# Last stage of a two-block transformer: weights scaled by ScalarE instead of GpSimd, fewer VectorE operations for queries and gates, and transposes and scores issued as one step

## The reference, cut to what matters

```python
def _stick_breaking(q, k, v):          # 16 heads of 64; blocks of 128 queries
        mask = kpos[None, :] < qpos[:, None]
        z = jnp.einsum('bhqd,bshd->bhqs', qb, k).astype(jnp.float32) * scale
        log_beta = jax.nn.log_sigmoid(z)
        log_1mb = jnp.where(mask, jax.nn.log_sigmoid(-z), 0.0)
        suffix = lax.cumsum(log_1mb, axis=3, reverse=True) - log_1mb
        a = jnp.where(mask, jnp.exp(log_beta + suffix), 0.0)
        return jnp.einsum('bhqs,bshe->bhqe', a.astype(v.dtype), v)

def _sb_layer(x, k, v, norm_g, w_in, w_out):
    proj = _rms(x, norm_g) @ w_in
    q, g = jnp.split(proj, [SB_W], axis=-1)
    o = _stick_breaking(q.reshape(...), k, v)
    o = o.reshape(b, s, SB_W) * jax.nn.silu(g)
    return x + o @ w_out
```

## Time and profile before

| | us |
|---|---|
| median of 3 runs (lowest, highest) | 2911.08 (2909.06, 2913.7) |
| the profiled execution, its own time | 2911.05 |
| its span, first to last instruction | 2909.2 |
| TensorE busy | 2843.3 (98%) |
| VectorE busy | 1676.3 (58%) |
| ScalarE busy | 1092.2 (38%) |
| GpSimd busy | 397.3 (14%) |
| mean granted clock of TensorE | 0.995 |

### The profile page before, as it was taken

One profiled execution on the slowest core, in us unless ns is written; L12 is line 12 of the kernel. 1 busy time (PEld: TensorE's weight loads), 2 busy tenths in 40 slices (PEclk: granted clock), 3 DMA queues, 4 the chain that ended last, 5 costly groups with the idle time before them and its releaser, 6 DMA issues.

```text
span 2909.2 us, 34967 instructions
## 1 busy us (share of the span) xinstructions
PE 2843.3 (98%) x14241; PEld 2363.5 (81%) x14241; DVE 1676.3 (58%) x2400; ACT 1092.2 (38%) x1699; POOL 397.3 (14%) x263
## 2 busy tenths in 40 slices
PE   8999999999999999999999999999999899899988
PEld 7888887888888888888887889888888787678777
DVE  5554357675464533555247776555533677768884
ACT  4322244554332322323234454422222444444442
POOL 2000111110100001000011220100001322154430
PEclk9999999999999999999999999999999999999999
DMA  4332332243233233332323233233323222131211
GB/s 141 101 95 94 95 88 73 66 127 106 87 94 97 88 101 98 101 95 87 105 71 92 68 108 118 80 109 95 101 91 98 70 64 69 47 88 59 72 59 51
DMA packets 302240, 258.08 MB, mean 89 GB/s; under 512 B 11367, under 2 KB 299904, under 8 KB 302080
## 3 DMA queue, kind: packets, MB, share of 16 engines
q1 hardware_dynamic: 300704, 254.76, 28.7%
q10 hardware_dynamic: 1024, 1.05, 0.2%
q0 software_dynamic: 352, 0.03, 0.0%
HBM read 252.66 MB, written 2.10 MB: 88 GB/s over the span
## 4 chain that ended last, share of the span: by engine, by line
PE 82%; DVE 10%; ACT 3%; issue 3%; POOL 2%; DMA 1%; ACTq 0%; SPq 0%; POOLq 0%; DVEq 0%
PE PS L1525 26%; PE PS L1527 25%; PE PS L1526 25%; DVE WL L2255 3%; PE PS L1531 2%; PE PS L1770 1%; DVE AF L2701 1%; DVE SM L2619 1%; ACT AF L2129 0%; PE PS L1623 0%; PE PS L1812 0%; PE PS L1811 0%; DVE AR L2711 0%; ACT WH L1872 0%; POOL SM L2869 0%
## 5 line engine op out<-in xcount | busy, mean ns | idle before, releaser
L2255 DVE TENSOR_TENSOR WL<-RAW,WH 128x1024 fp32r<-128x1024 f32 x480 | 617.9, 1293 | 572.9 <-ACT WH L1872 572.6
L1525 PE MATMUL PS<-XH,WL 128*128 128x512 f32 x2256 | 904.4, 401 | 2.9 <-DVE XL L2265 2.9
L1527 PE MATMUL PS<-XH,WH 128*128 128x512 f32 x2256 | 883.3, 392 | 0.0
L1526 PE MATMUL PS<-XL,WH 128*128 128x512 f32 x2256 | 882.1, 391 | 0.0
L1872 ACT ACTIVATE WH<-RAW 128x1024 fp32r<-128x1024 f32 x448 | 465.4, 1044 | 1005.9 <-PE PS L1527 994.6
L1525 PEld LDWEIGHTS PS<-XH,WL 128*128 128x128 f32 x2256 | 425.8, 189 | 101.5 <-issue 12.7
L1527 PEld LDWEIGHTS PS<-XH,WH 128*128 128x128 f32 x2256 | 425.2, 188 | 91.5
L1526 PEld LDWEIGHTS PS<-XL,WH 128*128 128x128 f32 x2256 | 426.3, 189 | 81.1
L1525 PE MATMUL PS<-AR,WL 128*128 128x512 f32 (+1 forms) x1216 | 465.3, 383 | 7.3 <-DVE SC L2599 3.5
L1527 PE MATMUL PS<-AR,WH 128*128 128x512 f32 (+1 forms) x1216 | 460.7, 379 | 0.0
L1526 PE MATMUL PS<-AR,WH 128*128 128x512 f32 (+1 forms) x1216 | 460.6, 379 | 0.0
(11 more groups left out here) (259 smaller groups left out, 3000.0 us busy)
## 6 DMA issues: line engine op xcount, KB each, us to landing
RAW<-in_w_ffn_gu_dram SPq DMA_DIRECT2D x176, 512.0 KB, 3.5
RAW<-in_w_ffn_down_dram SPq DMA_DIRECT2D x80, 512.0 KB, 3.4
RAW<-in_w_mix_in_dram SPq DMA_DIRECT2D x48, 512.0 KB, 4.0
RAW<-in_w_xkv_dram SPq DMA_DIRECT2D x32, 512.0 KB, 3.4
RAW<-in_a_w_in_dram SPq DMA_DIRECT2D x32, 512.0 KB, 4.2
RAW<-in_w_mix_out_dram SPq DMA_DIRECT2D x16, 512.0 KB, 3.4
RAW<-in_w_xq_dram SPq DMA_DIRECT2D x16, 512.0 KB, 4.1
RAW<-in_w_xo_dram SPq DMA_DIRECT2D x16, 512.0 KB, 3.4
```

The lines of the kernel that those rows point to most:

```text
L1525: pe.matmul(o, ll, rh, start=start, stop=False, skip_group_check=skip)
L1526: pe.matmul(o, lh, rl, start=False, stop=False, skip_group_check=skip)
L1527: return pe.matmul(o, lh, rh, start=False, stop=stop, skip_group_check=skip)
L2255: dve.tensor_tensor(l, raw_slot(n), F(h), ALU.subtract).then_inc(sg["wl"].up(n))
```

## The change

The gain scaling moves from GpSimd to ScalarE, as one activation per k tile with the gain as its per-partition factor: 8 operations of 128x128 for a strip, 4 of 128x256 for a unit of values or of others. For the queries of `sb` the factor of the position is no longer multiplied in before the eviction; it goes as factor of each row (RCOL, and its negative NB4) into the sigmoids. The two halves of the values' product are added into one bank, and the gate is one product of 128 rows. In all three attention stages the transposes and the following scores become one step of the side stream, and the rates of the side streams are lowered to the new count.

```diff
@@ -547,7 +547,8 @@
                     self.add("bt", (s, m), "ptr", "ph")
-                    yield
+                    if n >= 16:
+                        yield
                 if n < 16:
...
@@ -602,14 +603,14 @@
         self.add("ctr", (s,), "ctr", "cq")
-        side = self.stream(att(0, 4), 6.5 / 64)
+        side = self.stream(att(0, 4), 4.3 / 64)
         self.weave(self.flow(self.chain(conv("v", 0), conv("b", 0), qk("q", 1), qk("k", 1))), side)
...
             self.finish(side)
-            side = self.stream(att(4 * m, 4 * m + 4), 10.5 / 80)
+            side = self.stream(att(4 * m, 4 * m + 4), 6.3 / 80)
             self.weave(self.flow(self.chain(conv("c", m), conv("v", m), conv("b", m), qk("q", m + 1), qk("k", m + 1))), side)
         self.finish(side)
-        side = self.stream(att(12, 16), 10.5 / 80)
+        side = self.stream(att(12, 16), 6.3 / 80)
         self.weave(self.flow(self.chain(self.values(s, 1), conv("c", 3), conv("v", 3), conv("b", 3))), side)
...
@@ -861,7 +862,8 @@
                     self.later(4, "dtl", (s, m), "pl")
-                    yield
+                    if n >= 32:
+                        yield
                 if n < 32:
...
@@ -907,7 +909,7 @@
             main.append(gated(t))
-            side = self.stream(att(4 * t, 4 * t + 4), 9.4 / (80 if t in (2, 4) else 48))
+            side = self.stream(att(4 * t, 4 * t + 4), 5.3 / (80 if t in (2, 4) else 48))
             self.weave(self.flow(self.chain(*main)), side)
...
@@ -929,7 +931,7 @@
 
-        side = self.stream(att(28, 33), 10.4 / 33)
+        side = self.stream(att(28, 33), 6.3 / 33)
         self.weave(self.flow(opening()), side)
...
@@ -1014,6 +1016,9 @@
 
+        if step[0] == "gy":
+            for hh in range(2):
+                self.due("bps", (LAST, *step[1], hh))
         if any(x[1][:2] == step for x in self.soon):
...
@@ -1036,7 +1041,7 @@
 
-        self.add("bqe", (s, w, t), "et", "eh")
+        self.add("bqe", (s, w, t), *(() if s == LAST and w == "q" else ("et",)), "eh")
         self.later(6, "bql", (s, w, t), "el")
...
@@ -1084,7 +1089,7 @@
                 self.give(self.bank_of[s, t, 0], "gy", (t,))
-                self.give(b, "gy", (t,))
+                self.give(b, "bps", (s, t, 1))
                 self.later(9, "gl", (t,), "ol")
...
@@ -1127,10 +1133,10 @@
         self.add("barrier", (s,))
-        self.add("mq", (s,), "mask", "zero", "tri")
+        self.add("mq", (s,), "mask", "zero", "tri", "minus")
         for w, t in (("q", 0), ("k", 0), ("q", 1)):
             self.heads_in(s, w, t)
-        side = self.stream(att(0, 4), 6 / 64)
+        side = self.stream(att(0, 4), 4.3 / 64)
         self.weave(self.flow(self.chain(qk("k", 1), self.values(s, 0), gated(0))), side)
...
@@ -1139,7 +1145,7 @@
                 main.append(gated(t - 1))
-            side = self.stream(att(4 * t - 4, 4 * t), 10.5 / (32 + (32 if t % 2 else 0) + (16 if t < 7 else 0)))
+            side = self.stream(att(4 * t - 4, 4 * t), 6.3 / (32 + (32 if t % 2 else 0) + (16 if t < 7 else 0)))
             self.weave(self.flow(self.chain(*main)), side)
...
@@ -1150,7 +1156,7 @@
 
-        side = self.stream(att(28, 33), 13 / 56)
+        side = self.stream(att(28, 33), 8.2 / 56)
         self.weave(self.flow(opening()), side)
...
@@ -1813,7 +1819,7 @@
                 w.then_inc(sg["pv"].up(s, t, hh))
-                free[b] = [{"mix": ("yl", (s, t, hh)), "diff": ("dov", ("o", t)), "sb": ("gy", (t,))}[nm(s)]]
+                free[b] = [{"mix": ("yl", (s, t, hh)), "diff": ("dov", ("o", t)), "sb": ("pvs", (s, t, 1)) if hh else ("gy", (t,))}[nm(s)]]
                 free[b] = [sg[g].at(*key) for g, key in free[b]]
...
@@ -1874,6 +1880,14 @@
 
+            def scale(n):
+                g0 = units[n][2]
+                w = raw_slot(n)
+                on.wait_ge(*raw_ready(n))
+                for k in range(w.shape[1]):
+                    t = act.activation(w[:, k, :], w[:, k, :], ACT.Copy, scale=GA[:, g0 + k:g0 + k + 1])
+                t.then_inc(sg["wg"].up(n))
+
             def xh(s, m):
...
@@ -2154,7 +2168,10 @@
                 h, _, f = slot_qk(w, t)
-                on.wait_ge(*sg["et"].at(s, w, t))
+                if s == LAST and w == "q":
+                    on.wait_ge(*sg["mm"].at(((s, f"{w}{t}"), 0), 0, KT - 1))
+                else:
+                    on.wait_ge(*sg["et"].at(s, w, t))
                 if t > 1:
...
@@ -2167,8 +2184,10 @@
                     on.wait_ge(*sg["ptr"].at(s, n - 3))
-                act.activation(OM[n % 2][:, :, T - N:T], z, ACT.Sigmoid, scale=-1.0).then_inc(sg["exps"].up(s, n))
-                act.activation(BE[n % 3][:, :, T - N:T], z, ACT.Sigmoid).then_inc(sg["sbe"].up(s, n))
+                i = n % 4
+                on.wait_ge(*sg["minus"].at(s))
+                act.activation(OM[n % 2][:, :, T - N:T], z, ACT.Sigmoid, scale=NB4[:, i:i + 1]).then_inc(sg["exps"].up(s, n))
+                act.activation(BE[n % 3][:, :, T - N:T], z, ACT.Sigmoid, scale=RCOL[:, i:i + 1]).then_inc(sg["sbe"].up(s, n))
...
@@ -2347,6 +2366,8 @@
                     dve.memset(F(GONE[:, 0:384]), 0.0).then_inc(sg["zero"].up(s))
+                    on.wait_ge(*sg["rcol"].at(s))
+                    dve.tensor_scalar(NB4, RCOL, -1.0, None, ALU.mult).then_inc(sg["minus"].up(s))
                     on.wait_ge(*sg["mask"].at(s))
...
@@ -2466,9 +2487,9 @@
                 r = slice(64 * hh, 64 * hh + 64)
-                y = PS[P.bank_of[s, t, hh]][r, :]
                 on.wait_ge(*sg["pvx"].at(s, t, hh))
-                dve.tensor_tensor(y, y, F(YL[r, t, :]), ALU.add).then_inc(sg["pvs"].up(s, t, hh))
+                dve.tensor_tensor(PS[P.bank_of[s, t, 0]][r, :], PS[P.bank_of[s, t, hh]][r, :], F(YL[r, t, :]),
+                                  ALU.add).then_inc(sg["pvs"].up(s, t, hh))
...
@@ -2681,6 +2702,8 @@
             def bqe(s, w, t):
+                if s == LAST and w == "q":
+                    return
                 o = tile_bank(s, w, t)
...
@@ -2689,7 +2712,8 @@
                 on.wait_ge(*sg["eh"].at(s, w, t))
-                on.wait_ge(*sg["et"].at(s, w, t))
+                if s < LAST or w == "k":
+                    on.wait_ge(*sg["et"].at(s, w, t))
                 dve.scalar_tensor_tensor(l, tile_bank(s, w, t), f, F(h), ALU.mult, ALU.subtract).then_inc(sg["el"].up(s, w, t))
...
@@ -2724,11 +2748,9 @@
                 on.wait_ge(*sg["gu"].at(t))
-                for hh in range(2):
-                    r = slice(64 * hh, 64 * hh + 64)
-                    on.wait_ge(*sg["pvs"].at(LAST, t, hh))
-                    y = dve.tensor_tensor(ET[r, t % 2, :], ET[r, t % 2, :], PS[P.bank_of[LAST, t, hh]][r, :], ALU.mult)
-                y.then_inc(sg["gy"].up(t))
+                on.wait_ge(*sg["pvs"].at(LAST, t, 1))
+                e = ET[:, t % 2, :]
+                dve.tensor_tensor(e, e, PS[P.bank_of[LAST, t, 0]], ALU.mult).then_inc(sg["gy"].up(t))
...
@@ -2774,13 +2796,6 @@
                     pool.memset(F(h), 0.0).then_inc(sg["pad"].up(n))
-
-            def scale(n):
-                g0 = units[n][2]
-                w = raw_slot(n)
-                nk, nc_ = w.shape[1], w.shape[2]
-                on.wait_ge(*raw_ready(n))
-                pool.tensor_tensor(w, w, GA[:, g0:g0 + nk].unsqueeze(2).to_broadcast([128, nk, nc_]), ALU.mult).then_inc(sg["wg"].up(n))
...
```

4 lines of the change are left out of this document (2 added, 2 removed).

## The result

The changed kernel takes 2921.38 us (median of 5 runs, 2918.62 to 2923.75) against 2911.08 before: the ratio is 1.0035, 95% interval 1.0022 to 1.0047. So it is slower by a third of a per cent; I had forecast 2903 us. The profiled execution is at 2919.64 us, with a span of 2917.8.

The account below looks back on a forecast made before the run. TensorE was taken as the bound, its last-stage waits set by VectorE's in-order queue, which GpSimd's operations lengthen. Savings of -11, -4, -1 and costs of +5, +2, +1 made -8 against 2911.05 us: 2903 us, range 2890 to 2918.

Parts of the forecast that it names:

- Spacing in `diff`: In `diff`, transposes and scores in one step leave a shorter interval that just fits: +1 us (ends -6 and 6).
- `mix`: In `mix`, transposes and scores in one step were charged nothing, since TensorE hardly stands there.
- Waits for L2711: In the last stage, TensorE's waits for the low halves of the transposed probabilities fall from 14.0 to 3 us: -11.
- Clock: In the last stage, two thirds of 6 us lost to a granted clock of 0.97 go with the waits: -4 us.
- L2723: In the last stage, TensorE's wait of 3.1 us for this line shrinks by a shorter queue of VectorE: -1 us.
- ScalarE's load: In the last stage, 68 us more work on ScalarE costs 5 us of TensorE's time (ends 0 and 20).
- Opening: At the last stage's start, scalings waiting for their DMA stand before the last two XH: +2 us (ends -1 and 5).
- One gate product, factor in the sigmoids: In the last stage, VectorE saves 5.5 us by the gate and 5.5 by dropped query evictions.
- the first: Rival, 0.22: in the last stage ScalarE stands at weights not yet landed and blocks all behind it; slower, 2918 us.
- The second: Rival, 0.18: in the last stage waits move to transposes' eviction on ScalarE and use up the savings; no change, 2911 us.
- The third: Rival, 0.10: pairing also gains a third of TensorE's 21 us of idle in `diff`, and 2 us more waits; 2894 us.
- Over 25 us of idle on TensorE in `diff`: Sign that the forecast is wrong: TensorE idle in `diff` above 25 us, where it had 21 us before.

Follow-up runs that it names:

- `diff` apart: Changed kernel with transposes and scores of `diff` put back into steps of their own, at the rates of before: 2902.86 us, ratio to before 0.9968.
- the version with the values product later: Changed kernel, `diff` still paired but at the scores' old places (rate 9.4), values product one step later, behind an empty step: 2916.51 us, ratio 1.0011.
- `diff` paired wide: Changed kernel, `diff` still paired, at rate 4.7 in place of 5.3, so row groups 10.2 matmul units apart as before: 2920.69 us.

## Why the prediction was wrong

Step by step, by the terms of its sum:

- **Spacing in `diff`, +1 (ends -6 and 6): the step that failed.** It measured +18.6 in the profiles and 18 in the times, and alone turns the forecast around. I checked one chain, from the mask to the exps that free the score banks (3.4 us), against 3.1 us of matmuls, and found that "with the transposes' matmuls between, it just fits". It was never one chain. In the same interval VectorE and ScalarE also have the rotation of the q and k tiles (L2607 to L2629), the turned tile's low half (L2665) and the output's norm (L2677), and each ends at a matmul. Either half of the edit lets some of them come late: the closer spacing alone gives 331 us, the pairing alone at the old spacing 324 to 336, both 330, where before had 311. That each was just in time before is my reading of this, not a measurement. The term also had no part for the clock: of the 18.6 us, 9.4 are idle time of TensorE and 11.9 lower clock behind it, less 2.7 in the rest.
- **`mix`, 0:** -1.9 us each, -3.8 in sum. Mis-sized by a little, and in the gaining direction.
- **Waits for L2711, -11: the second step that failed.** 14.0 us (15.1 with the one at the values product) became 11.8. I laid the late L2711 to the scaling and to the place of the subtraction. The pairing alone leaves 16.7 us of these waits, and moving the scaling takes some 4 off. The subtraction ahead of L2711 is long under `bmul`, which stays, and the pairing makes the two meet more often, not less. Already in the earlier trace rows the one directly ahead of L2711 was under `bmul`. What the Trainium skill ("SBUF — State Buffer", section "Who interferes with whom") says of the shared port predicts that `bmul` goes on blocking L2255. The trace agrees: beside a `bmul` the subtraction took 3.41 us where its own time is 1.22. I used it for 3 us of waits and should have asked how often the two would meet. The waits have another releaser behind them too: VectorE's L2735 stood 17.4 us for ScalarE's eviction (L2198), where L2711 had stood 7.5.
- **Clock, -4:** the low clock in the rest of the last stage went from 6.8 to 1.9 us in the profiled executions. The pairing gets it without any other edit (0.5 with the last stage paired, 0.3 with `mix` too), though other executions with it have 3.9 to 5.9. It isn't tied to the sum of the waits as I had it: idle stayed at 22 us with the pairing alone. What fell with it is the length of the longest, from 3.1 to 2.1 us. So the size was nearly right, and the path that I gave for it was not.
- **L2723, -1:** 3.1 became 1.1 us, and so it does with the pairing alone.
- **ScalarE's load, +5 (ends 0 and 20):** no run measures it by itself. With ScalarE scaling the rest of the last stage is 2.3 to 4.4 us shorter, the relief of VectorE and the load of ScalarE together. Of TensorE's waits 2.3 us are for a line of ScalarE (L1776 <- L2190), and none was before. A strip takes 2.44 us, a unit of four 1.71. I had 2.1 and 1.56 from neighbouring rows. The estimate from the figures of the Trainium skill ("ScalarE: Activation LUTs", section "What ACT_TABLE_LOAD costs") was 2.4 and 1.7, and the trace agrees.
- **Opening, +2:** +3.2 and +3.3. Right in size and in its reason, the XH that stand behind a scaling; 1.7 of it is lower clock.
- **One gate product, factor in the sigmoids:** VectorE's busy time fell in all as forecast, to 226 us, but by 1.5 us for the factor where I had 5.5. No gain in time is shown.

Without its `diff` term the sum was -9, and the changed kernel with `diff` apart is at 2902.86 us against 2911.05 - 9 = 2902. That agreement is luck in good part: the -11 was mostly not there, and what stands in for it is the 3.8 us of `mix` that I had put at nothing, the load of 5 that I charged, and a little more of clock and L2723.

Of the rivals, the first had ScalarE idle for 20 us or more with the DMA of RAW, and it is: 18.7 + 2.9 us. But only the opening pays for it; that rival's 13.5 us in the periods are not there, since the rest of the stage got shorter. The second is right in its mechanism, since L2735 stands longer for its eviction on ScalarE (17.4 us against 7.5); but the last stage behind its norm gained 7 us all the same, most of it clock. The third, that `diff` gains, was the reverse of what happened; its own counter-argument, that the waits there are not for that chain, pointed at the other chains. "Over 25 us of idle on TensorE in `diff`" stood among the signs that I would be wrong, and it is 30.8.

Settled is that the edit of `diff` costs, that its spacing and its pairing each do by themselves, and at which lines TensorE then stands. Open is what causes the pairing's part: the waits of the values product are one (5 us of idle went with them), and the 6.7 us of idle that stay above the apart version (25.2 against 18.5) stand in the rotation's lines (L1633 <- L2628 with 5.7 us, L1541 <- L2611 with 3.5), without an experiment that takes them away.

## What to carry to other kernels

Where a stage runs at 93% of the bound engine with a hand-timed order, the price of moving one step is not read from the chain that the step belongs to: list every chain that ends at the bound engine in that interval, and check each against the new spacing. A change to several stages at once should be split by stage before it is judged: here the same edit was worth -2, -2 and -6 us in three stages and +18 in the fourth. And when an operation leaves an engine, its collisions and its share of the path are two things: here 19 us of VectorE's busy time went as forecast, and less than 2 us of TensorE's idle with them, since the collision ahead of the operation on the path was with another.

## What the runs showed of the hardware

- A stall of TensorE of one to four microseconds can be followed by a piece at 1.2 in place of 2.4 GHz, of some 4 us, also in a stage where TensorE is busy for 90% of the time. In the last stage before, four stalls of 2.5 to 3.1 us were followed by one each; in `diff` of the changed kernel stalls of 1.2 and 1.4 us were too, and elsewhere such stalls were not.
- These pieces go with most of the difference between executions of one kernel. The ten runs of the version with the values product later go from 2907.7 us (mean granted clock 0.994) to 2920.48 (0.990), and 0.004 of 2910 us is 12 of these 13; those with `diff` paired wide go from 2914.48 (0.995) to 2924.64 (0.991). A difference of 5 us between two profiles can be this alone.
- GpSimd's in-place multiplications lengthen VectorE's scans beside them: those of 128 columns took 1019 ns on average with the scaling on GpSimd and 503 without.
- Eight ScalarE operations of 128 columns with a factor from a column take 2.44 us together, 0.39 for one: each next one starts 0.29 us later (the changed kernel at 2667.94 us).
- An issue of a DMA by ScalarE takes 0.63 us, and behind four of them an eviction started 2.74 us after the operation before them had ended (2394.71 to 2397.45).
